# Gate/up and half of the input projection of a decoder step: two weight slots at once, matmuls alternating between two PSUM banks

## The chip, the core and the metric

The kernel runs on one core of a Trainium2 chip. The metric is the device time of one execution in microseconds (us), taken as the median of several runs. Engines are named as the profile names them: PE is TensorE (matmuls; its weight loads are PEld), DVE VectorE, ACT ScalarE, POOL GpSimd, SP SyncE, which here only starts transfers.

## What is computed

One inference step of a two-layer decoder on 320 tokens: a prompt of 256 and 8 sequences of 8 new tokens. Each layer does, on one residual stream x of width 1024:

```
x += 0.5 * swiglu(rmsnorm(x), w_gate1, w_up1, w_down1)      # gate/up 1, down 1
z  = rmsnorm(x) @ w_in                                      # input projection, 2048 columns
x += concat(A, B, C, D)(z) @ w_out                          # four mixers, output projection
x += 0.5 * swiglu(rmsnorm(x), w_gate2, w_up2, w_down2)      # gate/up 2, down 2

def rmsnorm(x, gain):
    return x * lax.rsqrt(jnp.mean(x * x, axis=-1) + RMS_EPS) * gain

def swiglu(x, w_gate, w_up, w_down):
    return (jax.nn.silu(x @ w_gate) * (x @ w_up)) @ w_down
```

The hidden width of the swiglu is 2816, that is 22 tiles of 128. Mixer A is attention with normed queries and keys over a paged cache, the others are pooling, a convolution and a spatial gate. All values are fp32.

## The kernel before

Activations lie feature-major: x is [128, 8 tiles, 320 tokens]. Every product of fp32 values is made from rounded parts: a weight tile is raw = w_hi + w_lo, the normed input is xg_hi + xg_lo, and PE adds hi by hi, hi by lo and lo by hi in PSUM, so each tile of 128 input features (a k-tile) costs three matmuls of 128 by 128 by 320.

Weights pass through four slots. A slot holds 8 k-tiles of one column of 128 output features (512 KB), in `raw`, `w_hi` and `w_lo`. SP loads a slot's `raw` (L328) once POOL has split the slot's last content; ACT rounds it into `w_hi` (`round_slot`, L807) once PE has released the slot (semaphore `slots`); POOL makes `w_lo` = raw - w_hi (L429, semaphore `split`); PE waits for `split`, does 24 matmuls and releases the slot with the last of them (`use_slot`). Each engine runs its own program in written order.

A layer goes through gate/up 1 (11 iterations of four slots: gate and up of two hidden tiles), down 1 (8 tiles of 66 matmuls, PSUM banks 4 and 5), the input projection (4 iterations), the mixers, the output projection (2), gate/up 2 (11) and down 2. In gate/up and projection, slot j writes PSUM bank j (`column`); before it, `bank_free` waits until DVE has taken the bank's last content (semaphore `taken`).

The norm is not applied to the input: the columns are computed from x * gain, and DVE multiplies what it takes from PSUM by 1/rms. The squares are summed over features by one matmul with a matrix of ones into bank 6 (`sum_squares`, L545), in the first iteration, behind column 1 for the first norm of a layer and behind column 0 for the second (projection) and the third (gate/up 2). ACT takes the root of it (L788) and only then turns to the `round_slot` of iteration 1; DVE inverts it. In the first iteration column 0 also waits, k-tile by k-tile, for `xg_lo` (DVE, L998), which follows from the residual sum of the stage before (DVE, L1045).

In gate/up ACT's order in an iteration is: round slot 0, silu of the first gate, round slot 1, round the first hidden tile, and the same with slots 2 and 3. In the projection ACT rounds the slots of iterations 1, 2 and 3 between steps on the queries and keys; behind slot 1 of iteration 3 stands the root of the query and key norm (L896), then DVE's reciprocal (L1152), which PE spreads over the partitions (`qk_spread`, L589) in the midst of iteration 3. SP loads the slots of iterations 2 and 3 each followed by four transfers of cache pages:

```
for j in range(4):
    load_slot(L, BASE_I, 2 + n, j, w8, ...)
    load_past(L, n * 4 + j)
```

Of the kernel before, what the change touches and what calls it, by code (L numbers as in the profile page):

```python
# [31 lines left out]
P = 128  # L32
# [3 lines left out]
TOK = SEQ + NS  # L36
# [7 lines left out]
DT = D_MODEL // P  # L44
# [51 lines left out]
def hybrid_decoder(nc, xT, w8, w11, gains, vecs, consts, pool_w, conv_pw, sp_wT, sp_b,  # L96
# [3 lines left out]
    with ctx:  # L100
        place = [16512]

        def sb(name, shape, dt=F32, at=None):
            n = 4
            for s in shape[1:]:
                n *= s
            offset = place[0] if at is None else at[0]
            t = nc.alloc_sbuf_tensor_at(name, shape, dt, offset=offset)
            end = offset + (n + 31) // 32 * 32
            if at is None:  # L110
                place[0] = end
                assert end <= 229344, (name, end)
            else:
                at[0] = end
                assert end <= at[1], (name, end, at[1])
            return t

        raw = sb("raw", [P, 4, 8 * P])
        w_hi = sb("w_hi", [P, 4, 8 * P], F32R)
        w_lo = sb("w_lo", [P, 4, 8 * P], F32R)  # L120
# [5 lines left out]
        xg_hi = sb("xg_hi", [P, DT, TOK], F32R)  # L126
        xg_lo = sb("xg_lo", [P, DT, TOK], F32R)
# [69 lines left out]
        bank = [ctx.enter_context(nc.psum_tensor(f"bank{i}", [P, 512], F32)) for i in range(8)]  # L197

        def sig(name, per_layer, head=0):
            return Signal(ctx.enter_context(nc.semaphore(name)), per_layer, head)  # L200
# [11 lines left out]
        split = sig("split", 4 * ITS, 4)  # L212
        slots = sig("slots", 4 * ITS, 4)
        taken = sig("taken", TILES, 4)
        xg_hi_ok = sig("xg_hi_ok", 3 * DT, DT)
        xg_lo_ok = sig("xg_lo_ok", 3 * DT, DT)
# [305 lines left out]
        def _(pe):  # L522
            pe.sem_inc(slots.sem, 4)

            def use_slot(L, base, i, j, out, k_tiles, in_hi, in_lo, first, last, before_k=None):

                pe.wait_ge(split.sem, L * split.per + (base + i) * 4 + (j + 1 + split.head))
                for n, k in enumerate(k_tiles):
                    if before_k:
                        before_k(n, k)  # L530
                    hi, lo = w_hi[:, j, n * P:(n + 1) * P], w_lo[:, j, n * P:(n + 1) * P]
                    pe.matmul(out, hi, in_hi[:, k, :], start=first and n == 0, stop=False)  # L532
                    pe.matmul(out, hi, in_lo[:, k, :], start=False, stop=False)  # L533
                    end = n == len(k_tiles) - 1
                    mm = pe.matmul(out, lo, in_hi[:, k, :], start=False, stop=last and end)  # L535
                mm.then_inc(slots.sem, 1)

            def bank_free(L, tile):

                pe.wait_ge(taken.sem, L * taken.per + tile + 1)  # L540

            def sum_squares(L, n):

                pe.wait_ge(summed.sem, L * summed.per + (n + 1) * (DT + 1))
                pe.matmul(bank[6][:, 0:TOK], ones[:, :], sumsq[:, :], start=True, stop=True).then_inc(norm_sum.sem, 1)  # L545

            def column(L, base, tile0, norm, i, j, first=False):

                bank_free(L, i * 4 + (tile0 + j))

                ready = (lambda n, k: pe.wait_ge(xg_lo_ok.sem, L * xg_lo_ok.per + norm * DT + k + 1)) if first and j == 0 else None
                use_slot(L, base, i, j, bank[j][:, 0:TOK], range(8), xg_hi, xg_lo, True, True, ready)
                if first and j == (1 if norm == 0 else 0):
                    sum_squares(L, norm)

            def columns(L, base, tile0, norm, i, first=False):
                for j in range(4):
                    column(L, base, tile0, norm, i, j, first)

            def down(L, base, tile0, ffn):  # L560
                with pe.Fori(0, IT_D // 2) as i2:
# [8 lines left out]
            def gate_up(L, base, tile0, norm):  # L570
                columns(L, base, tile0, norm, 0, first=True)
                with pe.Fori(1, IT_G) as i:
                    columns(L, base, tile0, norm, i)
# [165 lines left out]
            with pe.Fori(0, DEPTH) as L:  # L739
                gate_up(L, BASE_G1, T_G1, 0)  # L740
                down(L, BASE_D1, T_D1, 0)


                columns(L, BASE_I, T_I, 1, 0, first=True)
                columns(L, BASE_I, T_I, 1, 1)
                pe.wait_ge(small_in.sem, small_in.at(L, small_in.per))
                column(L, BASE_I, T_I, 1, 2, 0)
                column(L, BASE_I, T_I, 1, 2, 1)
                qk_sums(L)
                column(L, BASE_I, T_I, 1, 2, 2)  # L750
# [21 lines left out]
                with pe.Fori(0, IT_O) as i:  # L772
                    for j in range(4):
                        bank_free(L, i * 4 + (T_O + j))
                        counts = dict(MIX_ORDER)
                        ready = (lambda n, k: pe.wait_ge(mix_ok.sem, mix_ok.at(L, counts[k]))) if j == 0 else None
# [638 lines left out]
```

## Time and profile before

| | before |
|---|---|
| median of 3 runs | 1222.77 us (1222.68 to 1225.25) |
| profiled execution, span | 1226.1 us |
| PE busy | 1181.8 us, 96% |
| POOL busy | 818.7 us, 67% |
| DVE busy | 652.4 us, 53% |
| ACT busy | 540.7 us, 44% |

The median is over runs without a profile; the span is that of one profiled execution, from the first instruction to the last. Busy time is the time in which an engine has an instruction under way, over the whole span; in PE's case an instruction that runs at a lower clock counts for longer.

### The profile page before, as it was taken

What the parts mean: (1) busy time and instruction counts of PE and PEld (TensorE: products, weight loads), DVE (VectorE), ACT (ScalarE), POOL (GpSimd) and SP (SyncE); (2) the same over time, 40 slices, a digit from 0 to 9 for tenths busy, and PEclk for the clock granted to TensorE, in tenths of its full rate; (3) what the DMA queues carried; (4) which work ended last, traced back from release to release, by engine and by line L of the source; (5) the groups of instructions that cost most, each with busy time, mean ns of one, the idle gap of its engine ahead of it and who ended that gap; (6) DMA issues with size and microseconds to landing.
All of it is one profiled execution on the core that took longest, in us unless ns stands there. A gap on an engine that the chain in (4) does not pass through costs nothing.

```text
span 1226.1 us, 24298 instructions
## 1 busy us (share of the span) xinstructions
PE 1181.8 (96%) x7924; PEld 1151.3 (94%) x7924; DVE 652.4 (53%) x909; ACT 540.7 (44%) x795; POOL 818.7 (67%) x428
## 2 busy tenths in 40 slices
PE   5999999999996999999999999999999889999998
PEld 5999999998786999999999999999987879999998
DVE  6877772247855445432258767522777555445222
ACT  4444344434734444444444444444456344444444
POOL 4876767675844666667767776677557456666667
PEclk9999999999997999999999999999999979999999
DMA  8454435566294444435565444455562934444455
GB/s 250 155 161 147 153 110 153 161 181 197 76 99 145 147 146 153 151 111 152 155 185 162 148 151 142 120 154 172 181 196 70 131 113 154 152 142 136 132 151 169
DMA packets 85938, 182.75 MB, mean 149 GB/s; under 512 B 25467, under 2 KB 39171, under 8 KB 85891
## 3 DMA queue, kind: packets, MB, share of 16 engines
q1 hardware_dynamic: 85600, 181.07, 51.8%
q10 hardware_dynamic: 290, 1.10, 0.2%
q8 instruction: 24, 0.39, 0.1%
q14 instruction: 24, 0.19, 0.0%
HBM read 178.55 MB, written 3.58 MB: 149 GB/s over the span
## 4 chain that ended last, share of the span: by engine, by line
PE 44%; POOL 26%; issue 23%; DVE 2%; DMA 1%; POOLq 1%; SPq 1%; ACT 1%; DVEq 0%; ACTq 0%
POOL w_lo L429 25%; PE bank L532 14%; PE bank L533 14%; PE bank L535 14%; DMA raw<-in_w 1%; POOL win L465 1%; DVE sumsq L1006 0%; DMA x<-in_xT 0%; SPq L375 0%; ACT xg_hi L792 0%; POOLq L428 0%; POOL conv_y L450 0%; POOL tmp L447 0%; DVE xg_lo L998 0%; PE bank L736 0%
## 5 line engine op out<-in xcount | busy, mean ns | idle before, releaser
L429 POOL TENSOR_TENSOR w_lo<-raw,w_hi 128x1024 fp32r<-128x1024 f32 (+2 forms) x356 | 775.2, 2182 | 397.0 <-ACT w_hi L807 397.0
L532 PE MATMUL bank<-xg_hi,w_hi 128*128 128x320 f32 x1664 | 525.3, 316 | 36.0 <-DVE xg_lo L998 30.9
L807 ACT ACTIVATE w_hi<-raw 128x1024 fp32r<-128x1024 f32 (+2 forms) x356 | 342.4, 962 | 474.4 <-PE bank L535 421.3
L535 PE MATMUL bank<-xg_hi,w_lo 128*128 128x320 f32 x1664 | 519.2, 312 | 0.0
L533 PE MATMUL bank<-xg_lo,w_hi 128*128 128x320 f32 x1664 | 519.1, 312 | 0.0
L532 PEld LDWEIGHTS bank<-xg_hi,w_hi 128*128 128x128 f32 x1664 | 316.8, 190 | 44.1 <-DVE xg_lo L998 34.5
L533 PEld LDWEIGHTS bank<-xg_lo,w_hi 128*128 128x128 f32 x1664 | 317.3, 191 | 1.0 <-issue 0.4
L535 PEld LDWEIGHTS bank<-xg_hi,w_lo 128*128 128x128 f32 x1664 | 316.8, 190 | 0.0
L532 PE MATMUL bank<-h_hi,w_hi 128*128 128x320 f32 x704 | 217.5, 309 | 0.0
L533 PE MATMUL bank<-h_lo,w_hi 128*128 128x320 f32 x704 | 217.5, 309 | 0.0
L535 PE MATMUL bank<-h_hi,w_lo 128*128 128x320 f32 x704 | 217.5, 309 | 0.0
L1028 DVE TENSOR_TENSOR h_lo<-tmp,h_hi 128x320 f32 (+1 forms) x88 | 175.9, 1998 | 73.6 <-ACT h_hi L815 73.6
L532 PEld LDWEIGHTS bank<-h_hi,w_hi 128*128 128x128 f32 x704 | 132.1, 188 | 0.0
L533 PEld LDWEIGHTS bank<-h_lo,w_hi 128*128 128x128 f32 x704 | 132.1, 188 | 0.0
L535 PEld LDWEIGHTS bank<-h_hi,w_lo 128*128 128x128 f32 x704 | 132.1, 188 | 0.0
L1045 DVE SCALAR_TENSOR_TENSOR x<-bank,x 128x320 f32 x48 | 23.4, 487 | 203.1 <-PE bank L535 203.1
L1023 DVE TENSOR_TENSOR tmp<-bank,rms 128x320 f32<-128x320 f32 x88 | 42.9, 488 | 150.3 <-PE bank L535 150.2
L998 DVE SCALAR_TENSOR_TENSOR xg_lo<-x,gain,xg_hi (+1 forms) x56 | 72.6, 1306 | 73.2 <-ACT xg_hi L792 73.2
L811 ACT ACTIVATE tmp<-tmp 128x320 f32<-128x320 f32 x88 | 40.8, 463 | 88.1 <-DVE tmp L1021 88.1
L1096 DVE SCALAR_TENSOR_TENSOR conv_y<-conv_in,vec,conv_y 128x64 f32<-128x64 f32 x88 | 62.6, 752 | 2.9
L1026 DVE TENSOR_TENSOR tmp<-tmp 128x320 f32<-128x320 f32 x88 | 51.4, 584 | 8.1 <-ACT tmp L811 5.8
L815 ACT ACTIVATE h_hi<-tmp 128x320 f32 (+1 forms) x88 | 41.2, 468 | 18.9 <-DVE tmp L1026 18.9
(167 smaller groups left out, 732.3 us busy)
## 6 DMA issues: line engine op xcount, KB each, us to landing
raw<-in_w SPq DMA_DIRECT2D x228, 512.0 KB, 3.9
raw<-in_w SPq DMA_DIRECT2D x64, 384.0 KB, 3.1
raw<-in_w SPq DMA_DIRECT2D x64, 320.0 KB, 2.9
k_all<-in_cache_kT SPq DMA_DIRECT2D x32, 128.0 KB, 3.0
v_past<-in_cache_v SPq DMA_DIRECT2D x32, 128.0 KB, 2.8
x<-in_xT SPq DMA_DIRECT2D x2, 640.0 KB, 5.8
cst<-in_consts ACTq DMA_DIRECT2D x1, 997.0 KB
out_yT<-x SPq DMA_DIRECT2D x1, 960.0 KB, 7.6
```

The costliest lines, as they stand in the source:

```text
L429: pool.tensor_tensor(w_lo[:, j, 0:count * P], raw[:, j, 0:count * P], w_hi[:, j, 0:count * P].bitcast(F32), ALU.subtract).then_inc(split.s ...
L532: pe.matmul(out, hi, in_hi[:, k, :], start=first and n == 0, stop=False)
L533: pe.matmul(out, hi, in_lo[:, k, :], start=False, stop=False)
L535: mm = pe.matmul(out, lo, in_hi[:, k, :], start=False, stop=last and end)
L807: act.activation(w_hi[:, j, 0:count * P], raw[:, j, 0:count * P], ACT.Copy).then_inc(split_hi.sem, 1)
L811: act.activation(tmp[:, 2 + m, :], tmp[:, m, :], ACT.Silu).then_inc(silu_ok.sem, 1)
L815: act.activation(h_hi[:, bass.ds(i * 2 + m, 1), :].rearrange("p a t -> p (a t)"), tmp[:, 6 + m, :], ACT.Copy).then_inc(h_hi_ok.sem, 1)
L998: dve.scalar_tensor_tensor(out=xg_lo[:, bass.ds(d, 1), :].rearrange("p a t -> p (a t)"), in0=one, scalar=gain[:, bass.ds(gain_col, 1)], in ...
L1023: dve.tensor_tensor(tmp[:, 4 + m, :], bank[2 * m + 1][:, 0:TOK], rms[:, :], ALU.mult).then_inc(taken.sem, 1)
L1026: dve.tensor_tensor(tmp[:, 6 + m, :], tmp[:, 2 + m, :], tmp[:, 4 + m, :], ALU.mult).then_inc(h_ok.sem, 1)
L1028: dve.tensor_tensor(h_lo[:, bass.ds(i * 2 + m, 1), :].rearrange("p a t -> p (a t)"), tmp[:, 6 + m, :], h_hi[:, bass.ds(i * 2 + m, 1), :].b ...
L1096: dve.scalar_tensor_tensor(out=y, in0=window, scalar=weight, in1=y, op0=ALU.mult, op1=ALU.add).then_inc(batch_taps.sem, 1)
```

## The change

Columns are computed two at a time (`column_pair`): PE waits for both banks and for the split of the second slot (which comes after that of the first), and then, for each k-tile, does the six matmuls of both columns in turn: hi by hi into bank j and into bank j + 1, hi by lo into both, lo by hi into both. Both slots are released by the pair's last two matmuls. In gate/up all iterations do so, in the projection iterations 0 and 1 (those through `columns`); iterations 2 and 3 call `column` as before. In the first iteration the pair of columns 0 and 1 waits for `xg_lo` by k-tile, and the sum of squares follows this pair for all three norms.

```diff
--- before.py
+++ after.py
@@ -544,18 +544,36 @@
                 pe.wait_ge(summed.sem, L * summed.per + (n + 1) * (DT + 1))
                 pe.matmul(bank[6][:, 0:TOK], ones[:, :], sumsq[:, :], start=True, stop=True).then_inc(norm_sum.sem, 1)
 
-            def column(L, base, tile0, norm, i, j, first=False):
+            def column(L, base, tile0, norm, i, j):
 
                 bank_free(L, i * 4 + (tile0 + j))
-
-                ready = (lambda n, k: pe.wait_ge(xg_lo_ok.sem, L * xg_lo_ok.per + norm * DT + k + 1)) if first and j == 0 else None
-                use_slot(L, base, i, j, bank[j][:, 0:TOK], range(8), xg_hi, xg_lo, True, True, ready)
-                if first and j == (1 if norm == 0 else 0):
+                use_slot(L, base, i, j, bank[j][:, 0:TOK], range(8), xg_hi, xg_lo, True, True)
+
+            def column_pair(L, base, tile0, norm, i, j, first=False):
+
+                outs = []
+                for e in range(2):
+                    bank_free(L, i * 4 + (tile0 + j + e))
+                    outs.append(bank[j + e][:, 0:TOK])
+                pe.wait_ge(split.sem, L * split.per + (base + i) * 4 + (j + 2 + split.head))
+                for k in range(DT):
+                    if first and j == 0:
+                        pe.wait_ge(xg_lo_ok.sem, L * xg_lo_ok.per + norm * DT + k + 1)
+                    cols = slice(k * P, (k + 1) * P)
+                    for e in range(2):
+                        pe.matmul(outs[e], w_hi[:, j + e, cols], xg_hi[:, k, :], start=k == 0, stop=False)
+                    for e in range(2):
+                        pe.matmul(outs[e], w_hi[:, j + e, cols], xg_lo[:, k, :], start=False, stop=False)
+                    for e in range(2):
+                        mm = pe.matmul(outs[e], w_lo[:, j + e, cols], xg_hi[:, k, :], start=False, stop=k == DT - 1)
+                        if k == DT - 1:
+                            mm.then_inc(slots.sem, 1)
+                if first and j == 0:
                     sum_squares(L, norm)
 
             def columns(L, base, tile0, norm, i, first=False):
-                for j in range(4):
-                    column(L, base, tile0, norm, i, j, first)
+                for j in range(0, 4, 2):
+                    column_pair(L, base, tile0, norm, i, j, first)
 
             def down(L, base, tile0, ffn):
                 with pe.Fori(0, IT_D // 2) as i2:
```

PE's program in the loop of gate/up 1, before: the start of column 0 and, behind the dots, the start of column 1. The waits for `taken` are for the bank, those for `split` for the slot.

```order
L527 ISA [waits taken]
L532 MATMUL bank0<-xg_hi_55,w_hi_50 128x320 [waits split]
L533 MATMUL bank0<-xg_lo_56,w_hi_50 128x320
L535 MATMUL bank0<-xg_hi_55,w_lo_51 128x320
...
L540 ISA
L527 REGISTER_ALU [waits taken]
L532 MATMUL bank1<-xg_hi_55,w_hi_50 128x320 [waits split]
L533 MATMUL bank1<-xg_lo_56,w_hi_50 128x320
L535 MATMUL bank1<-xg_hi_55,w_lo_51 128x320
```

The same place with the change: the start of the pair of columns 0 and 1.

```order
L540 ISA [waits taken]
L558 ISA [waits taken]
L564 MATMUL bank0<-xg_hi_55,w_hi_50 128x320 [waits split]
L564 MATMUL bank1<-xg_hi_55,w_hi_50 128x320
L566 MATMUL bank0<-xg_lo_56,w_hi_50 128x320
L566 MATMUL bank1<-xg_lo_56,w_hi_50 128x320
L568 MATMUL bank0<-xg_hi_55,w_lo_51 128x320
L568 MATMUL bank1<-xg_hi_55,w_lo_51 128x320
L564 MATMUL bank0<-xg_hi_55,w_hi_50 128x320
L564 MATMUL bank1<-xg_hi_55,w_hi_50 128x320
```

The waits of column 1 now stand ahead of column 0's first matmul, and each matmul writes another bank than the one before it.

PE's program at the start of the projection, before: the end of column 0 (its last k-tile waits for `xg_lo`), the sum of squares, and the start of column 1.

```order
L532 MATMUL bank0<-xg_hi_55,w_hi_50 128x320 [waits xg_lo_ok]
L533 MATMUL bank0<-xg_lo_56,w_hi_50 128x320
L535 MATMUL bank0<-xg_hi_55,w_lo_51 128x320
L544 REGISTER_ALU
L545 MATMUL bank6<-sumsq_75,ones_60 128x320 [waits summed]
L540 REGISTER_ALU
L527 REGISTER_ALU [waits taken]
L532 MATMUL bank1<-xg_hi_55,w_hi_50 128x320 [waits split]
L533 MATMUL bank1<-xg_lo_56,w_hi_50 128x320
```

The same place with the change: the last k-tile of the pair of columns 0 and 1, the sum of squares, and the start of the pair of columns 2 and 3.

```order
L564 MATMUL bank0<-xg_hi_55,w_hi_50 128x320 [waits xg_lo_ok]
L564 MATMUL bank1<-xg_hi_55,w_hi_50 128x320
L566 MATMUL bank0<-xg_lo_56,w_hi_50 128x320
L566 MATMUL bank1<-xg_lo_56,w_hi_50 128x320
L568 MATMUL bank0<-xg_hi_55,w_lo_51 128x320
L568 MATMUL bank1<-xg_hi_55,w_lo_51 128x320
L544 REGISTER_ALU
L545 MATMUL bank6<-sumsq_75,ones_60 128x320 [waits summed]
L540 REGISTER_ALU
L540 REGISTER_ALU [waits taken]
L558 REGISTER_ALU [waits taken]
L564 MATMUL bank2<-xg_hi_55,w_hi_50 128x320 [waits split]
```

The sum has moved from the end of column 0 behind all of column 1. At the start of gate/up 2 the rows move in the same way, with the waits for that stage.

## Rows read from the trace of the kernel before

**Rows 1.** Page, first part: busy time, share of the span and instructions of each engine.

```profile
PE 1181.8 (96%) x7924; PEld 1151.3 (94%) x7924; DVE 652.4 (53%) x909; ACT 540.7 (44%) x795; POOL 818.7 (67%) x428
```

**Rows 2.** Timeline of POOL in gate/up 2: start us, us, engine, line, operation, [idle before <-releaser].

```profile
399.66 2.41 POOL L429 TENSOR_TENSOR w_lo<-raw,w_hi 128x1024 fp32r<-128x1024 f32 x1 [1.11 <-ACT w_hi L807]
...
526.38 2.41 POOL L429 TENSOR_TENSOR w_lo<-raw,w_hi 128x1024 fp32r<-128x1024 f32 x1 [1.11 <-ACT w_hi L807]
```

**Rows 3.** Timeline of PE in down 1.

```profile
187.18 0.31 PE L533 MATMUL bank<-h_lo,w_hi 128*128 128x320 f32 x1
...
235.58 0.31 PE L533 MATMUL bank<-h_lo,w_hi 128*128 128x320 f32 x1
```

**Rows 4.** L429 (duration ns min/median/max, first and last start); timelines PE, ACT, POOL from 401.8.

```profile
L429 POOL TENSOR_TENSOR w_lo<-raw,w_hi x356: 1567/2404/2672, 6.3 to 1222.8; 128x1024 fp32r<-128x1024 f32 x114, 128x768 fp32r<-128x768 f32 x32, 128x640 fp32r<-128x640 f32 x32
...
401.84 0.31 PE L532 MATMUL bank<-xg_hi,w_hi 128*128 128x320 f32 x1
...
402.04 1.06 ACT L807 ACTIVATE w_hi<-raw 128x1024 fp32r<-128x1024 f32 x1 [2.10 <-PE bank L535]
...
403.18 2.40 POOL L429 TENSOR_TENSOR w_lo<-raw,w_hi 128x1024 fp32r<-128x1024 f32 x1 [1.12 <-ACT w_hi L807]
```

**Rows 5.** Timelines of PE and POOL, gate/up 1 of layer 0.

```profile
25.36 0.81 PE L545 MATMUL bank<-sumsq,ones 128*128 128x320 f32 x2 [1.26 <-DVE sumsq L1006]
...
26.15 0.31 PE L533 MATMUL bank<-xg_lo,w_hi 128*128 128x320 f32 x1
...
34.18 7.92 POOL L429 TENSOR_TENSOR w_lo<-raw,w_hi 128x1024 fp32r<-128x1024 f32 x3
```

**Rows 6.** Timelines of POOL and PE, start of the projection, layer 0.

```profile
248.21 4.79 POOL L429 TENSOR_TENSOR w_lo<-raw,w_hi 128x1024 fp32r<-128x1024 f32 x2 [0.21 <-ACT w_hi L807]
...
255.75 0.41 PE L532 MATMUL bank<-xg_hi,w_hi 128*128 128x320 f32 x1 [1.24 <-DVE xg_lo L998]
...
256.30 0.70 PE L545 MATMUL bank<-sumsq,ones 128*128 128x320 f32 x2
```

**Rows 7.** Timelines of POOL, SP, ACT, PE: projection, layer 0; then ACT, PE, layer 1.

```profile
258.59 2.41 POOL L429 TENSOR_TENSOR w_lo<-raw,w_hi 128x1024 fp32r<-128x1024 f32 x1 [3.23 <-ACT w_hi L807]
...
261.26 0.33 SPq L328 DMA_DIRECT2D raw<-in_w  x1
...
287.92 0.66 SPq L328 DMA_DIRECT2D raw<-in_w  x1
...
292.30 1.06 ACT L807 ACTIVATE w_hi<-raw 128x1024 fp32r<-128x1024 f32 x1 [4.70 <-DMA raw<-in_w]
...
298.09 2.42 PE L589 MATMUL bank<-tmp,cst 8*128 8x320 f32 x8
...
896.61 1.06 ACT L807 ACTIVATE w_hi<-raw 128x1024 fp32r<-128x1024 f32 x1 [5.29 <-DMA raw<-in_w]
...
901.73 2.42 PE L589 MATMUL bank<-tmp,cst 8*128 8x320 f32 x8
```

**Rows 8.** Windows: us, busy (x) of PE PEld DVE ACT POOL, PEclk, DMA share, GB/s.

```profile
301.46:304.80 3.34, 3.34 (x14) 3.34 (x14) 3.25 (x12) 1.59 (x2) 0.48 (x1) 0.51 0.56 173
...
379.60:387.44 7.84, 2.19 (x7) 1.39 (x7) 5.96 (x7) 3.75 (x7) 4.92 (x2) 0.51 0.46 140
...
387.44:393.30 5.86, 5.86 (x20) 5.47 (x21) 2.82 (x3) 3.74 (x4) 0.62 (x1) 0.50 0.12 43
...
500.00:600.00 100.00, 100.00 (x684) 100.00 (x684) 31.42 (x42) 42.46 (x60) 67.66 (x37) 1.00 0.47 138
```

**Rows 9.** Timelines of POOL, DVE, PE: gate/up 2 of layer 0.

```profile
372.36 4.97 POOL L429 TENSOR_TENSOR w_lo<-raw,w_hi 128x1024 fp32r<-128x1024 f32 x2 [10.14 <-ACT w_hi L807]
...
377.60 0.48 DVE L1045 SCALAR_TENSOR_TENSOR x<-bank,x 128x320 f32 x1
...
387.44 0.63 PE L532 MATMUL bank<-xg_hi,w_hi 128*128 128x320 f32 x1 [3.29 <-DVE xg_lo L998]
...
388.40 1.27 PE L545 MATMUL bank<-sumsq,ones 128*128 128x320 f32 x2
```

## The prediction

> **What bounds the kernel now.** I read the first part of the profile's page, then the timeline of PE with its idle times, then POOL, ACT, DVE and SP around each of them. PE is busy for 1181.8 of 1226.1 us, POOL for 818.7 [rows 1]: what can be won is PE's idle time or the spacing of its matmuls. The spacing is steady. A row of POOL's gate/up loop comes again after nine iterations, 126.72 us later [rows 2]: 14.080 us an iteration, and with 96 matmuls 146.7 ns each. A row of the down loop comes again after five tiles, 48.40 us later [rows 3]: 9.680 us a tile, with 66 matmuls again 146.7 ns. So the two parts that remain are the columns in steady state, where the change acts on nearly every matmul, and six places where PE waits or will wait: the first iteration of each gate/up (four times) and of the projection (twice).
>
> **Bank alternation.** The change puts 4608 matmuls in pairs of banks (4 gate/ups of 11 iterations with 96, 2 projections with 2 iterations). The trace of before has no k-by-k alternation, so its price is bounded. Consecutive matmuls of before nearly all write the same bank, and a column changes bank once in 24, a down tile once in 66; both have 146.7 ns [rows 2, 3], so a bank change costs or saves nothing that shows. From the other side: 320 columns at 2.4 GHz are 133.3 ns, and if writing one bank twice in a row cost all the rest, 13.3 ns, alternation would give back 13.3 x 4608 = 61 us. I take 0, the value of the rows; 61 us is a rival. The rows don't exclude a little either way: 0.01 us in 48.40 is 0.03 ns a matmul, on a difference of 1/24 - 1/66 = 0.027 bank changes a matmul, so about 1 ns a change stays open, 5 us on the whole.
>
> **Refill of a pair in steady state.** Both slots of a pair are released together and have 48 matmuls, 7.04 us, until they are wanted. Let T be PE's first matmul after the release. ACT's w_hi starts 0.20 later (401.84 to 402.04), takes 1.06, POOL's w_lo starts 0.08 behind it (403.18) [rows 4]: T+1.34. The second w_hi is done by T+2.8 (ACT's silu of 0.5 between them), so POOL runs two w_lo back to back: median 2.40, at most 2.67 each [rows 4]. With 0.1 to PE slot 1 is ready at T+6.2 to T+6.8. That fits 7.04 us with 0.2 to 0.8 to spare: cost 0, as long as a w_lo stays under 2.8 us. DVE's steps lie in the same 7 us, and their last product is not wanted before the down stage.
>
> **First iteration of gate/up 1 (both layers).** Here iteration 1 waits for a chain that starts only at the matmul of the norm's sum: root, table load, w_hi, then four w_lo in one run. In layer 0 the sum stands at 25.36, columns 2 and 3 start at 26.00 (0.15 ahead of the row at 26.15) and, 48 matmuls on, end at 33.04. Slot 0 is split before that, so before there was no wait. The pair wants slot 1 too: POOL's third w_lo starts at 34.18, so its second ends just there, and PE starts at 34.28 [rows 5]: **+1.24**. The chain is 34.28 - 25.36 = 8.92 us. Layer 1 has the same three rows from 629.11 on, and the same **+1.24**. The start of the kernel costs 0 to 0.3: PE begins later (it needs slot 1), but the sum waits for DVE anyway.
>
> **Projection (both layers).** Before, column 0 runs to its last k-tile and waits 1.24 us for xg_lo until 255.75; it had begun 21 matmuls before, at 251.27. Slot 1 was ready at 253.00 minus 2.4 (two w_lo from 248.21) [rows 6]. The pair starts at 251.27 as well, has 42 matmuls for the same seven k-tiles, reaches the last at 257.4, and waits no more: PE wins 1.39. But the sum of the norm moves from between column 0 and 1 (256.30) behind the pair: 251.27 + 7.04 = 258.32, **2.02 later**. Behind it in ACT's queue stand root and w_hi of iteration 1, behind that POOL's w_lo (258.59 to 261.00), and SP's load of the next raw block waits for that (261.26). From there SP works off one load after the other with the cache pages between, until the last block of concern at 287.92, 26.7 us later without a wait for anything else; ACT waits 4.70 us for it (292.30), then come table load, root, DVE's reciprocal, and PE's spread at 298.09. In layer 1 the wait is 5.29 us (896.61) and the spread follows 5.12 us on, at 901.73 [rows 7]. So the whole chain shifts by 2.02. In layer 1 PE was just waiting for it: +2.02. In layer 0 the chain was ready at 292.30 + 5.12 = 297.42 and PE came 0.67 later: **+1.35** there, **+2.02** in layer 1. The 1.39 that PE won is swallowed: it now stands idle before the spread for 1.35 + 1.39 = 2.7 us, in layer 1 for 3.4. Everything behind (mixers, SP's loads for the output projection and gate/up 2) follows PE and SP and shifts alike.
>
> **The clock there.** In before the spread runs at full clock (2.42 us for x8) [rows 7] and the granted clock falls behind it, to 0.51 (1.2 GHz) for 3.34 us [rows 8]. Bounds for the new idle time: nothing (the fall comes anyway), or a fall ahead of the spread, which then takes twice 2.34. I take one such fall, in layer 1 where the idle time is longer: **+2.34**.
>
> **First iteration of gate/up 2 (both layers).** Before, PE starts column 0 when the first w_lo is there (372.36 + 2.48) and then waits for xg_lo three times, the last time until 387.44; the sum stands at 388.40, column 1 follows at half clock, and iteration 1 begins at 401.84 [rows 4, 9]. The pair starts when slot 1 is split (377.33) and bank 1 is empty (DVE's residual at 377.60 + 0.48): 378.1. Its first 42 matmuls, 20 of them at half clock (5.86 us) [rows 8] and 22 at 146.7 ns, end at 387.2, still ahead of the last xg_lo, which doesn't hang on PE. So the sum comes at 388.3, as before, but column 1 is already done in PE's idle time. Iteration 1 then starts with the chain of gate/up 1: 388.3 + 8.92 = 397.2, **-4.6**. In layer 1 the same rows give **-4.3**. If the clock is low again behind the sum, as in before, the last k-tile and columns 2 and 3 are the limit: then -2.9 each.
>
> **Sum.** 1.24 + 1.24 + 1.35 + 2.02 + 2.34 - 4.6 - 4.3 = -0.7 us on the profiled execution of 1226.1 us. The median of the runs shown is 1222.77, 3.3 us below that span; I apply the difference to the median: **1222.0 us**, no change. I count as change what is over 0.2%, 2.45 us, about what a measurement of this kernel can tell from none.
>
> **Rivals.**
> *No fall of the clock before the spread* (its 3.34 us at half clock behind the spread merely come earlier): -3.0, 1219.8 us. For it speaks that in before PE's idle times of 1.2 us pass without a fall [rows 6]; against it that 3.4 us is longer than those.
> *The sum's delay is absorbed*: if SP's loads make up the 2.02, PE keeps its 1.39 twice and no fall comes: 2.48 - 2.78 - 8.9 = -9.2, 1213.6 us. Against it: ACT waits for the last of these loads for over 4 us in both layers [rows 7].
> *Alternating banks shorten the spacing*: -61, 1161 us. Only the distance from 133.3 ns speaks for it; equal spacing in rows 2 and 3 against it.
> *Low clock at all places*: a fall ahead of the spread in both layers and low clock behind both sums of gate/up 2: 2.48 + 3.37 + 4.68 - 5.8 = +4.7, 1227.5 us, slower. For it: at 379.60 to 393.30 the clock was 0.50 to 0.51 [rows 8], with PE waiting as it will again.
> *The refill doesn't fit*, the one that ends well on the other side: from a mean w_lo of 2.8 us on, each 0.1 us more costs 0.2 in each of 80 steady pairs (4 x 10 iterations, two pairs each, are 80). With 3.0 us that is 0.4 x 80 = +32, 1255 us. For it: two w_lo now run back to back while DVE works off both takes of the pair at once; against it the maximum of 2.67 in all 356 [rows 4], in which such runs of two to four are (372.36, 34.18). The Trainium skill (SBUF — State Buffer, section on SBUF's two separate sides) has VectorE operations with two SBUF inputs and GpSimd operations exclude each other for a whole instruction, whichever starts first; by that rule a w_lo could start late by one DVE step, and the spare 0.2 to 0.8 us would be gone where steps of 0.5 us fall badly.
> *The clock oscillates in steady state*: a fall costs 2.9 us (20 matmuls in 5.86 us where 2.93 would do) [rows 8]; one in each of 44 iterations would be +129, 1352 us. Against it: from 500 to 600 us, with a bank change every 24 matmuls, the clock is 1.00 and PE 100% busy [rows 8]. The Trainium skill (TensorE: Matmul & The Clock Gate, section on a second failure mode, the cycling through PSUM banks) tells of a kernel that cycled through banks and, by small idle times between its groups of matmuls, kept losing the clock; the trace agrees so far only that idle PE and low clock go together.
>
> **Chances.** Forecast, with its small variants inside 0.2%: 0.52. No fall: 0.17. Delay absorbed: 0.06. Banks: 0.04. Low clock at all places: 0.10. Refill: 0.09. Oscillation: 0.02. Faster by over 0.2%: 0.17 + 0.06 + 0.04 = 0.27; within: 0.52; slower: 0.21. The range takes in the forecast, the case without a fall and the case of low clock, 0.79 in all. Of the 5 us that the rows leave open for the banks I give a quarter, 1.3, to its low end: 1219.8 - 1.3 = 1218.5, since nothing measured points there. Its high end is 1227.5 and the 0.3 of the kernel's start: 1227.8.
>
> **What would show it.** Right: steady iterations still 14.08 us apart; PE idle 1.2 us before iteration 1 of gate/up 1; no wait for xg_lo in the projection, its sum 2.0 us later, and PE idle 2.7 and 3.4 us before the spread; iteration 1 of gate/up 2 about 9 us behind the sum. Wrong: an idle time in every pair with POOL as releaser, a spacing other than 146.7 ns, a spread that isn't late.

## The result and the profile after

The changed kernel takes 1228.86 us (median of 6 runs, 1226.51 to 1231.47), the kernel before 1222.80 (median of 6, 1221.16 to 1225.25): a ratio of 1.0048 with a 95% interval of 1.0034 to 1.0062. It is slower by 6 us, where no change was forecast, and lies 1 us above the range.

The page of the changed kernel begins with the line that answers to [rows 1]:

```profile
PE 1177.4 (96%) x7924; PEld 1147.8 (94%) x7924; DVE 734.5 (60%) x909; ACT 533.3 (43%) x795; POOL 832.1 (68%) x428
```

PE has the same matmuls and is busy 4.4 us less, since less of its work falls into low clock (mean granted clock 0.993, before 0.983); DVE is busy 82 us more with the same 909 instructions. The span is 1226.8 us, beside 1226.1 before: the two profiled executions are nearly alike, and the runs differ by 6 us. That is the first thing to explain.

The waits of PE in the changed kernel (engine, operation and line, waited for: us in total, times, longest us):

```profile
PE bank L564 <- POOL w_lo L429: 21.9, 6, 15.8
PE bank L564 <- DVE x L1063: 8.3, 2, 5.0
PE bank L564 <- DVE xg_lo L1016: 4.2, 2, 2.8
PE bank L532 <- DVE qk L1077: 3.2, 2, 1.6
PE bank L532 <- DVE tmp L1039: 2.8, 4, 0.7
PE bank L607 <- DVE tmp L1170: 2.0, 2, 1.1
```

Of the first line 15.8 is the start of the kernel. New against before are a wait in front of each down stage (DVE tmp, four times 0.7), one in the projection (DVE qk, twice 1.6), and the wait for the spread (L607, twice 1.0).

In steady state nothing waits. POOL in gate/up 1, timeline as in [rows 2], and PE in gate/up 2, window as in [rows 8]:

```profile
63.70 5.04 POOL L429 TENSOR_TENSOR w_lo<-raw,w_hi 128x1024 fp32r<-128x1024 f32 x2 [1.99 <-ACT w_hi L825]
70.73 5.04 POOL L429 TENSOR_TENSOR w_lo<-raw,w_hi 128x1024 fp32r<-128x1024 f32 x2 [2.00 <-ACT w_hi L825]
...
420.00:520.00 100.00, 100.00 (x684) 100.00 (x683) 71.22 (x58) 40.92 (x58) 70.56 (x29) 1.00 0.47 149
```

Two w_lo take 5.04 us and a pair of them comes every 7.03 us: a pair of columns takes the 7.04 us of before, and PE is 100% busy at a clock of 1.00.

At the start of gate/up 1 (as [rows 5]) and of down 1, timelines of PE and DVE:

```profile
25.43 0.74 PE L545 MATMUL bank<-sumsq,ones 128*128 128x320 f32 x2
...
34.25 0.56 PE L564 MATMUL bank<-xg_hi,w_hi 128*128 128x320 f32 x2 [1.04 <-POOL w_lo L429]
...
174.85 0.46 PE L568 MATMUL bank<-xg_hi,w_lo 128*128 128x320 f32 x2
...
175.20 0.49 DVE L1039 TENSOR_TENSOR tmp<-bank,rms 128x320 f32<-128x320 f32 x1 [1.84 <-PE bank L568]
...
175.99 0.41 PE L532 MATMUL bank<-h_hi,w_hi 128*128 128x320 f32 x1 [0.68 <-DVE tmp L1039]
```

Iteration 1 follows the sum by 8.82 us (8.92 forecast). The down stage then waits for DVE's take of the last pair: its first matmul comes at 175.99, where the two of 174.85 would let it start at 175.14. Sum to down takes 150.56 us in the changed kernel, 148.48 before (25.36 to 173.84): 2.1 us a gate/up, not 1.24.

In the projection, timelines of PE, POOL and ACT as in [rows 6, 7], layer 0 and the last two rows layer 1:

```profile
253.53 0.46 PE L564 MATMUL bank<-xg_hi,w_hi 128*128 128x320 f32 x2
...
260.57 0.70 PE L545 MATMUL bank<-sumsq,ones 128*128 128x320 f32 x2
...
262.86 2.42 POOL L429 TENSOR_TENSOR w_lo<-raw,w_hi 128x1024 fp32r<-128x1024 f32 x1 [5.24 <-ACT w_hi L825]
...
283.99 0.41 PE L532 MATMUL bank<-xg_hi,w_hi 128*128 128x320 f32 x1 [1.60 <-DVE qk L1077]
...
297.08 1.06 ACT L825 ACTIVATE w_hi<-raw 128x1024 fp32r<-128x1024 f32 x1 [4.98 <-DMA raw<-in_w]
...
302.19 2.42 PE L607 MATMUL bank<-tmp,cst 8*128 8x320 f32 x8 [1.07 <-DVE tmp L1170]
...
904.05 3.31 PE L607 MATMUL bank<-tmp,cst 8*128 8x320 f32 x8 [0.97 <-DVE tmp L1170]
907.28 0.63 PE L532 MATMUL bank<-xg_hi,w_hi 128*128 128x320 f32 x1
```

From the pair's first matmul the sum comes 7.04 us on (before 256.30 - 251.27 = 5.03), the w_lo 9.33 (7.32), the spread 48.66 (46.82): the spread is late by 1.84 us. PE stood idle for 1.60 us on the way and for 1.07 us ahead of the spread, 2.67 in all, as forecast (2.7), though not all of it where forecast; in layer 1 it was 1.6 and 0.97, where 3.4 was forecast.

The clock behind the spread, windows as in [rows 8]:

```profile
304.40:309.00 4.60, 4.60 (x21) 4.46 (x21) 4.44 (x14) 2.03 (x2) 2.23 (x2) 0.63 0.68 214
907.28:912.00 4.72, 4.72 (x19) 4.72 (x19) 4.45 (x15) 2.18 (x2) 1.37 (x2) 0.50 0.58 182
```

In gate/up 2 of layer 0, timeline of PE as in [rows 9]:

```profile
379.91 0.90 PE L564 MATMUL bank<-xg_hi,w_hi 128*128 128x320 f32 x2 [5.04 <-DVE x L1063]
...
389.15 0.56 PE L564 MATMUL bank<-xg_hi,w_hi 128*128 128x320 f32 x2 [1.35 <-DVE xg_lo L1016]
...
390.13 0.70 PE L545 MATMUL bank<-sumsq,ones 128*128 128x320 f32 x2
...
398.99 0.56 PE L564 MATMUL bank<-xg_hi,w_hi 128*128 128x320 f32 x2 [1.12 <-POOL w_lo L429]
```

PE waits for bank 1 until 379.91, the clock is full when the sum comes (1.00 in windows from 384 to 399), and iteration 1 follows it by 8.86 us, where it was 13.44 (388.40 to 401.84). In layer 1 it follows by 9.41 us, where it was 13.18.

### The profile page after: what moved, and what is told of

Its sections match the earlier page's. It is cut to its first block, busy times and chain, and to the rows that moved or that the text cites. A ratio compares the mean times of both kernels' runs of the same rounds, so it can differ in the third digit from the quotient of the medians.

```text
span 1226.8 us, 24202 instructions
## 1 busy us (share of the span) xinstructions
PE 1177.4 (96%) x7924; PEld 1147.8 (94%) x7924; DVE 734.5 (60%) x909; ACT 533.3 (43%) x795; POOL 832.1 (68%) x428
## 4 chain that ended last, share of the span: by engine, by line
POOL 44%; issue 35%; PE 18%; POOLq 2%; DMA 0%; ACT 0%; DVEq 0%; ACTq 0%; DVE 0%; SPq 0%
POOL w_lo L429 41%; PE bank L564 4%; PE bank L566 4%; PE bank L568 4%; PE bank L532 2%; PE bank L533 2%; PE bank L535 2%; POOL win L465 1%; POOL conv_y L450 1%; POOL tmp L447 1%; POOLq L428 0%; DMA x<-in_xT 0%; POOLq L504 0%; POOLq L506 0%; ACT xg_hi L810 0%
## 5 line engine op out<-in xcount | busy, mean ns | idle before, releaser
L429 POOL TENSOR_TENSOR w_lo<-raw,w_hi 128x1024 fp32r<-128x1024 f32 (+2 forms) x356 | 788.7, 2230 | 384.2 <-ACT w_hi L825 383.8
L564 PE MATMUL bank<-xg_hi,w_hi 128*128 128x320 f32 x1536 | 355.4, 313 | 34.3 <-POOL w_lo L429 21.9
L568 PE MATMUL bank<-xg_hi,w_lo 128*128 128x320 f32 x1536 | 352.1, 311 | 0.0
L566 PE MATMUL bank<-xg_lo,w_hi 128*128 128x320 f32 x1536 | 352.1, 311 | 0.0
L564 PEld LDWEIGHTS bank<-xg_hi,w_hi 128*128 128x128 f32 x1536 | 258.6, 189 | 37.9 <-issue 27.0
L566 PEld LDWEIGHTS bank<-xg_lo,w_hi 128*128 128x128 f32 x1536 | 258.5, 189 | 0.0
L568 PEld LDWEIGHTS bank<-xg_hi,w_lo 128*128 128x128 f32 x1536 | 258.2, 189 | 0.0
L1044 DVE TENSOR_TENSOR tmp<-tmp 128x320 f32<-128x320 f32 x88 | 189.5, 2153 | 45.2 <-ACT tmp L829 45.2
L1046 DVE TENSOR_TENSOR h_lo<-tmp,h_hi 128x320 f32 (+1 forms) x88 | 151.6, 1723 | 73.5 <-ACT h_hi L833 73.5
L1086 DVE SCALAR_TENSOR_TENSOR bank<-conv_in,vec,bank 128x256 f32<-128x256 f32 x116 | 46.5, 483 | 0.3 <-DVE bank L1086 0.3
L532 PE MATMUL bank<-xg_hi,w_hi 128*128 128x320 f32 x128 | 43.3, 339 | 3.4 <-DVE qk L1077 3.2
```

What stands on the lines that cost most here:

```text
L429: pool.tensor_tensor(w_lo[:, j, 0:count * P], raw[:, j, 0:count * P], w_hi[:, j, 0:count * P].bitcast(F32), ALU.subtract).then_inc(split.s ...
L564: pe.matmul(outs[e], w_hi[:, j + e, cols], xg_hi[:, k, :], start=k == 0, stop=False)
L566: pe.matmul(outs[e], w_hi[:, j + e, cols], xg_lo[:, k, :], start=False, stop=False)
L568: mm = pe.matmul(outs[e], w_lo[:, j + e, cols], xg_hi[:, k, :], start=False, stop=k == DT - 1)
L1044: dve.tensor_tensor(tmp[:, 6 + m, :], tmp[:, 2 + m, :], tmp[:, 4 + m, :], ALU.mult).then_inc(h_ok.sem, 1)
L1046: dve.tensor_tensor(h_lo[:, bass.ds(i * 2 + m, 1), :].rearrange("p a t -> p (a t)"), tmp[:, 6 + m, :], h_hi[:, bass.ds(i * 2 + m, 1), :].b ...
```

## The experiments

Three groups of kernels ran, each group on one chip beside the kernel before, whose medians there were 1218.93, 1219.19 and 1220.50 us. Ratios are to the kernel before of the same group. Only the second group has a run of the changed kernel; elsewhere a kernel is compared with it by their ratios (1.0048 above, 1.0045 in the second group).

**The kernel before once more.**

> The kernel before once more. Theory 1 (fixed waits at stage changes make the changed kernel slower, against a gain at the start of gate/up 2 that is as large as the clock is low there): the profiled execution of before that the prediction used was itself a long one; a second one has a span near 1220.7 us, 2.1 below the median as with the changed kernel, and less than 13.6 us of low clock at the start of gate/up 2 of each layer. Rival: the second one is again near 1226 us with 13.6 us of low clock in each layer; then profile and runs differ by themselves for before, and its rows stand for its runs.

1218.95 us, 1.0001 (0.9987 to 1.0014); the profiled execution took 1217.38 us with a span of 1215.3. In every profiled execution here that has a time, the time is some 2.1 us more than the span (2.0 to 2.4; 1228.91 and 1226.8 for the changed kernel). The span of 1226.1 on which the prediction was built thus stands for some 1228.2 us, an estimate by this difference, above the slowest run of before beside it (1225.25). Theory 1 holds: it was a long execution; of the 72 executions of before in the three groups the longest spans 1224.6 us. The new profile in its turn is of a short one, 1.6 us below its median, on a chip whose median is 3.9 us below the first, so the two profiles lie further apart than two typical executions. Windows of the new one, behind the two spreads and behind the sum of gate/up 2:

```profile
300.80:304.00 3.20, 3.20 (x22) 3.17 (x22) 3.04 (x12) 0.80 (x1) 0.66 (x1) 1.00 0.56 186
898.20:902.00 3.80, 3.80 (x27) 3.61 (x28) 3.64 (x14) 1.71 (x2) 0.96 (x2) 1.00 0.64 213
...
386.00:390.00 4.00, 4.00 (x29) 4.00 (x28) 3.13 (x4) 2.70 (x4) 1.82 (x1) 1.00 0.01 2
```

And its timeline of PE at that place:

```profile
383.90 1.27 PE L545 MATMUL bank<-sumsq,ones 128*128 128x320 f32 x2
...
395.89 0.31 PE L532 MATMUL bank<-xg_hi,w_hi 128*128 128x320 f32 x1
```

No low clock behind the spread, where [rows 8] has 3.34 us of it, and sum to iteration 1 takes 11.99 us, not 13.44: the clock is full from 386.00 on, 2.1 us behind the sum, where [rows 8] still has it low 4.9 us behind. The other half of the expectation, less than 13.6 us of low clock, is met too: windows of 1 us each add up to 10 us in either layer. Most of the difference lies elsewhere. From the spread to the sum of gate/up 2 the first profile takes 90.31 us (298.09 to 388.40) in layer 0 and 88.00 in layer 1, the second 85.42 and 83.34: 9.55 of the 10.8 us by which the spans differ. Rows of the second (its spread), of the first (that sum in layer 1), and PE's waits for w_lo in the first and in the second:

```profile
298.48 2.42 PE L589 MATMUL bank<-tmp,cst 8*128 8x320 f32 x8
...
989.73 1.27 PE L545 MATMUL bank<-sumsq,ones 128*128 128x320 f32 x2
...
PE bank L532 <- POOL w_lo L429: 5.1, 3, 2.1
...
PE bank L532 <- POOL w_lo L429: 1.8, 1, 1.8
```

The first profile has two waits for w_lo more, of 2.1 and 1.3 us, each at the start of gate/up 2, and the low clock behind the spread costs it 1.5 us in each layer (24.77 us from the spread to the end of iteration 3, 23.23 in the second). The rest I have not taken apart. Among all twelve profiles that stretch is longest in the first, 178.3 us for both layers; the others have 168.8 to 177.0.

**Pairs without alternation.**

```diff
+                if not (first and j == 0):
+                    for e in range(2):
+                        for k in range(DT):
...
+                    mm.then_inc(slots.sem, 2)
+                    return
```

> The changed kernel, but in every pair except the first of a stage the 24 matmuls of the first column come ahead of the 24 of the second (no alternation); waits and releases stay at the pair's start and end. Theory 1: alternation neither costs nor saves; same as the changed kernel, 1228.9 us within 1.5, iterations 14.08 us apart. Rival (each alternating matmul costs about 1.3 ns, 6 us over 4608): near 1223 us.

1224.53 us, 1.0044 (1.0028 to 1.0059), as the changed kernel in the next group (1.0045). POOL's w_lo come 7.04 us apart, as with alternation. Alternating banks neither cost nor saved anything that shows.

**Single columns in the projection.**

```diff
             def columns(L, base, tile0, norm, i, first=False):
+                if norm == 1:
+                    for j in range(4):
...
+                        if first and j == 0:
+                            sum_squares(L, norm)
+                    return
```

> The changed kernel with single columns in the projection (the sum of squares again behind column 0). Theory 1: the spread comes 1.8 us earlier in each layer, 3.6 us less: 1225.3 us; DVE's take ahead of iteration 2 no longer keeps PE waiting 1.6 us. Rival (a cost in each alternating matmul): 384 of 4608 matmuls, 0.5 us less, 1228.4 us.

1219.10 us, 1.0004 (0.9991 to 1.0018): 0.4%, 5 us, less than the changed kernel, where 3.6 was expected. The waits for DVE's take and the spread are gone, and so is the low clock behind the spread.

**No wait of the first down tile for the last takes.**

```diff
+                def tile(i, e, wait):
+                    if wait:
+                        pe.wait_ge(taken.sem, L * taken.per + i + (tile0 - 2 + 1 + 4))
...
+                for e in range(2):
+                    tile(e, e, e > 0)
```

> The changed kernel, but the first tile of each down stage does not wait for DVE's takes of the last gate/up pair (it writes bank 4, which gate/up doesn't use; the later tiles wait as before). Theory 1: four waits of 0.7 us go, 2.8 us less: 1226.1 us. Rival: something else is late next there (the split of the first down slots, or h), and nothing changes: 1228.9 us.

1219.58 us, 1.0004 (0.9991 to 1.0017), 5 us less where 2.8 was expected. PE at the start of down 1:

```profile
175.23 0.46 PE L568 MATMUL bank<-xg_hi,w_lo 128*128 128x320 f32 x2
175.52 0.31 PE L532 MATMUL bank<-h_hi,w_hi 128*128 128x320 f32 x1
```

The next matmul follows with no gap. Nothing else is late there, so each of these waits costs the whole gap of 0.85 us (175.14 to 175.99), 3.4 in all; the other 1.8 us are within what the intervals leave open.

**The changed kernel once more.**

> The changed kernel once more, beside the three below on one chip, to have its time and profile there: 6 us (0.5%) above the kernel before. All theories agree.

1224.95 us, 1.0045 (1.0026 to 1.0064).

**The sum inside the pair.**

```diff
+                    if first and j == 0 and norm == 1 and k == 6:
+                        sum_squares(L, norm)
```

> The changed kernel, but in the projection's first pair the sum of squares stands ahead of the pair's seventh k-tile instead of behind the pair. Theory 1 (the late sum delays ACT's w_hi and through it SP's loads and the spread, and the idle time there lets the clock fall): the spread comes some 1.6 us earlier in each layer and no low clock follows it; 3.5 to 6 us less than the changed kernel, at most 0.2% above the kernel before. Rival (the DVE multiplications that POOL's w_lo now holds up, and the take of 1.6 us behind them, delay the spread by themselves): the spread stays late, less than 1.5 us gained.

1224.63 us, 1.0048 (1.0027 to 1.0068): nothing gained. ACT and PE in layer 0:

```profile
259.99 0.53 ACT L808 ACTIVATE root<-bank,stat 128x320 f32<-128x320 f32 x1 [3.95 <-PE bank L545]
261.61 1.06 ACT L827 ACTIVATE w_hi<-raw 128x1024 fp32r<-128x1024 f32 x1 [1.08 <-PE bank L570]
...
302.82 2.42 PE L609 MATMUL bank<-tmp,cst 8*128 8x320 f32 x8 [1.24 <-DVE tmp L1172]
```

The root comes early, but w_hi then waits 1.08 us for PE: slot 0 itself is released only at the pair's end. My theory named the wrong event. The rival (the DVE multiplications of the projection, which POOL's w_lo hold up) fits the time as well; the last experiment tells the two apart.

**Single columns in iteration 1 of gate/up.**

```diff
+                for j in range(4):
+                    column(L, base, tile0, norm, 1, j)
+                with pe.Fori(2, IT_G) as i:
```

> The changed kernel with single columns in iteration 1 of every gate/up (pairs in iteration 0 and from 2 on). Theory 1: iteration 1 waits for one split slot only, which is there in time; the waits of 1.0 to 1.2 us ahead of iteration 1 go in all four gate/ups: 4 to 5 us less than the changed kernel. Rival (a wait for the second slot just moves on to iteration 2): nothing gained.

1220.19 us, 1.0008 (0.9994 to 1.0023), 4.6 us less than the changed kernel's 1224.95 beside it. Iteration 1 starts without a wait, and no wait appears at iteration 2.

**One pair only, at the start of gate/up 2.**

```diff
             def columns(L, base, tile0, norm, i, first=False):
+                if first and norm == 2:
+                    column_pair(L, base, tile0, norm, i, 0)
+                for j in range(2 if first and norm == 2 else 0, 4):
+                    column(L, base, tile0, norm, i, j, first)
```

> The kernel before with one pair only: columns 0 and 1 of the first iteration of gate/up 2, the sum behind the pair. Theory 1: column 1 is hidden in the time in which PE waits for xg_lo, and nothing else changes: 3.5 us less in each layer, 7 us (0.6%) faster than the kernel before. Rival (what limits there is the arrival of the weights, which a pair waits for twice, or the low clock): within 2 us of the kernel before.

1211.30 us, 0.9938 (0.9925 to 0.9951): 7.9 us faster than the kernel before. PE in layer 0:

```profile
373.49 0.56 PE L567 MATMUL bank<-xg_hi,w_hi 128*128 128x320 f32 x2 [2.87 <-DVE x L1067]
...
382.72 0.56 PE L567 MATMUL bank<-xg_hi,w_hi 128*128 128x320 f32 x2 [1.27 <-DVE xg_lo L1020]
...
383.69 0.70 PE L545 MATMUL bank<-sumsq,ones 128*128 128x320 f32 x2
383.99 0.55 PE L532 MATMUL bank<-xg_hi,w_hi 128*128 128x320 f32 x1
...
391.26 0.31 PE L532 MATMUL bank<-xg_hi,w_hi 128*128 128x320 f32 x1
```

The sum stands where it does in the kernel before (383.90), and iteration 1 follows it by 7.57 us in place of 11.99: column 1 (3.52 us) is hidden, and the clock is full behind the sum (48 matmuls from 383.99 take 7.27 us).

**Three edits at once.** Single columns in the projection and in iteration 1, and down's first tile without the wait.

> The changed kernel with three edits at once: single columns in the projection, single columns in iteration 1 of each gate/up, no wait of down's first tile for the takes of the last pair. Pairs stay in iteration 0 and in iterations 2 to 10 of each gate/up. Theory 1 (the changed kernel loses only at these places, and pairs in steady state cost and give nothing): as fast as the kernel before with one pair at the start of gate/up 2, 0.6% (7 to 8 us) faster than the kernel before. Rival (the steady pairs cost something of their own, or a wait that goes moves on): no more than 4 us faster than the kernel before.

1211.26 us, 0.9927 (0.9912 to 0.9942): as fast as one pair alone, with pairs in nine of eleven iterations of every gate/up. Both versions beat the kernel before; of the two, the single pair is the smaller edit.

**Late release of slot 0.** In the projection's first iteration columns 0 to 3 release 0, 2, 1 and 1 slots.

```diff
+                                 (0, 2, 1, 1)[j] if first else 1)
```

> The changed kernel with single columns in the projection and the sum behind column 0, as before the change, but in the projection's first iteration slot 0 is released only with slot 1, at the end of column 1 (3.5 us later). If the late release of slot 0 is enough to delay ACT's w_hi, SP's loads and the spread: the spread comes 2.9 and 3.5 us later than with single columns alone, and the time is 6 to 10 us above that kernel's (0.5 to 0.8% above the kernel before). If only the place of the sum matters: as single columns alone, within 1.5 us of the kernel before.

1228.06 us, 1.0061 (1.0042 to 1.0080). ACT, DVE and PE in layer 0:

```profile
259.17 0.53 ACT L816 ACTIVATE root<-bank,stat 128x320 f32<-128x320 f32 x1 [3.66 <-PE bank L546]
262.69 1.06 ACT L835 ACTIVATE w_hi<-raw 128x1024 fp32r<-128x1024 f32 x1 [2.99 <-PE bank L535]
...
270.13 1.14 DVE L1160 TENSOR_TENSOR conv_in<-tmp 128x256 f32<-128x256 f32 x1
...
302.81 3.48 PE L617 MATMUL bank<-tmp,cst 8*128 8x320 f32 x7 [2.52 <-DVE tmp L1180]
```

With the projection's columns, their order and the sum as before the change, the release alone delays w_hi by 3 us, PE then waits 2.52 us for the spread, and the kernel is 7.6 us slower than the kernel before, some 7 us (0.57%) slower than single columns alone. The spread comes 2.56 and 2.45 us later than there, counted from the projection's first matmul (2.9 and 3.5 expected). The late release is enough, and the delay doesn't go through DVE's multiplications: only one of the four is held up here, by 0.7 us, and PE doesn't wait for DVE ahead of iteration 2. Nor are they on the way to the spread in the changed kernel: DVE stands idle for 6.2 us there ahead of its reciprocal, and ACT, for which it waits, has itself waited 4.98 us for a load (297.08).

## Why the prediction was wrong

**Two terms of the sum failed: a wait put at nothing, 3.4 us, and the gain in gate/up 2, of -8.9 us, which is about 3.3 too large.** The wait is for DVE. Of its steps the prediction says that "their last product is not wanted before the down stage"; but as soon as a down stage begins, the take of the last gate is wanted, and PE stands still for it, 0.85 us in each of four places. The gain was read from one execution of before. The runs give it another size: one pair alone gains 7.9 us at that place, and the wait for the second slot ahead of iteration 1 takes back about half of the 4.6 us that single columns there are worth in four gate/ups, so 5.6 is left (an estimate from these medians). The two make 6.7 of the 6.8 us between the forecast change of -0.7 and the measured one of +6.1, a closer match than medians that are good to 1.5 or 2 us warrant.

What let the second through is the last step: "3.3 us below that span; I apply the difference to the median". A span lies some 2.1 us *below* the time of its execution, so the one at hand was 5.4 us longer than the median (1228.2 against 1222.8), and a part of the gain that was read from it was one that the median never had to give. That the span lay above all three times shown was a sign that I read as a constant offset. By the two profiles that part is 1.7 us (13.44 and 13.18 us against 11.99 and 12.93 in the two layers); another 0.5 is the chain in layer 1 (9.41 for 8.92), and the rest of the 3.3 stays open. Most of the 5.4 lay between the spread and the sum of gate/up 2, where the change was not expected to gain anything.

Against that execution the change came out at +0.7 us (1226.8 - 1226.1), 1.4 from the forecast, but that is luck. From the sums to the down stages the changed kernel was 4.2 us worse than forecast (+2.07 and +2.15 in gate/up 1, -3.61 and -2.81 in gate/up 2), and from the spread to the sum of gate/up 2 it was 3.7 us better (-2.37 and +1.01 for the +2.34 of the clock), since before was long there.

**Bank alternation, 0**: right, by the pairs without alternation. **Refill, 0**: right; two w_lo take 5.04 of every 7.04 us, and with the 1.34 ahead of them and 0.1 behind some 0.5 us are to spare. The rival of a refill that doesn't fit, and that of an oscillating clock, fall.

**Gate/up 1, +1.24**: right at iteration 1 (34.25 for 34.28). Missing was the wait named above. Down's first tile waits for a count of DVE's takes that includes the gate of the last pair. It was taken during the last column before; now both columns of the pair end together, and PE stands still for DVE: 0.85 us in each of four places, 3.4 us. The count is stricter than bank 4 needs.

**Projection, +1.35 and +2.02**: the delay was right in size (+1.84 in layer 0; +1.80 in layer 1, 904.05 - 855.45 against 901.73 - 854.93), and the cause was half right. I named the sum; the release of slot 0 moves by the same 2.02 us and is enough by itself, while the sum moved ahead by itself gains nothing (1.0048). And PE's 1.39 us went to another wait than I said: it stood idle 1.60 us ahead of iteration 2 for DVE's take, not only before the spread. There DVE's multiplications took 2.46 and 2.44 us, under POOL's w_lo, timelines of DVE and POOL in the changed kernel:

```profile
269.34 5.05 POOL L429 TENSOR_TENSOR w_lo<-raw,w_hi 128x1024 fp32r<-128x1024 f32 x2 [1.69 <-ACT w_hi L825]
...
269.65 2.46 DVE L1150 TENSOR_TENSOR conv_in<-tmp 128x256 f32<-128x256 f32 x1
272.03 2.44 DVE L1151 TENSOR_TENSOR conv_in<-tmp 128x64 f32<-128x64 f32 x1
```

and in the kernel before (second profile), where POOL starts later than they end:

```profile
269.02 0.42 DVE L1132 TENSOR_TENSOR conv_in<-tmp 128x256 f32<-128x256 f32 x1
269.36 0.22 DVE L1133 TENSOR_TENSOR conv_in<-tmp 128x64 f32<-128x64 f32 x1
...
270.01 2.42 POOL L429 TENSOR_TENSOR w_lo<-raw,w_hi 128x1024 fp32r<-128x1024 f32 x1 [1.99 <-ACT w_hi L807]
```

Each of the two slow ones lasts about as long as a w_lo. The Trainium skill (SBUF — State Buffer, section on SBUF's two separate sides) says that whichever of the two starts first holds the shared ports for the whole instruction; the traces agree, 0.42 us against 2.46. I had looked for what this does to POOL only, and it is DVE that pays.

**The clock there, +2.34**: misplaced, and its size depends on the execution. The spread itself was slow once (3.31 us in layer 1), and the low clock behind it came in both layers of the changed kernel, none in the second profile of before and none with single columns in the projection. From the spread to the end of iteration 3 the changed kernel takes 24.78 and 26.36 us: 4.7 us in all above the second profile of before, 1.6 above the first. By medians, delay and clock together are right: 5.7 forecast, about 5 given back by single columns. What the low clock goes with can be counted over all twelve profiles: it lies in that stretch in 13 of the 14 layers in which PE stood idle ahead of the spread (by 0.3 to 2.5 us), and in 2 of the 10 in which it didn't, both in the first profile of before. One pair alone, which leaves the projection as it was, had it in the one layer in which PE waited there, for 0.49 us. No run shows what made it fall without such a wait.

**Gate/up 2, -4.6 and -4.3**: the mechanism was right, and the chain from sum to iteration 1 too (8.86 for 8.92). The size rested on 13.44 and 13.18 us of before, which are 11.99 and 12.93 in the other execution; against that the pair wins 3.1 and 3.5, and down's wait takes 0.85 of each. The experiment with one pair shows the full gain of 7.9 us, because there iteration 1 needs one slot and comes 7.57 us behind the sum, not 8.86.

The account by experiments, in us from the changed kernel on: projection about 5, down's wait about 5 (3.4 by the traces), iteration 1 4.6, in sum 15; all three at once gave 1.0045 - 0.9927 = 1.2%, 14.4 us. What is left, some 8 us faster than the kernel before, is the gain of gate/up 2.

## What to carry to other kernels

A pair that waits for two buffers and releases both at its end changes nothing in steady state and everything at the edges: look at each first and last iteration for what waited for the first buffer alone, for a release that moves, and for counts that include the pair's last product. Use such a pair only where the second half fills a wait that is there already. And hold the profiled execution's own time against the runs before a sum is built on it: if it is the longest of all, part of what can be gained in it is not there in the others.

## What the runs showed of the hardware that I had not expected

The clock behind an idle stretch came back at different times in two executions of the kernel before with the same instructions: 4.9 us or more behind the sum of gate/up 2 in the one, 2.1 or less in the other, which made 1.45 us (13.44 and 11.99 us to iteration 1). And with POOL's w_lo in runs of two DVE was busy for 734.5 us in place of 652.4 with the same 909 instructions: the product of gate and up (L1026, now L1044), whose two inputs both lie in SBUF, took 2153 ns in place of 584 on average. All nine profiles with pairs in the steady iterations of gate/up have DVE busy for 723 to 737 us, the three without for 646 to 652. PE, which waits for DVE only at the edges, lost nothing by it in steady state.
